# A fused two-block transformer kernel: experts of the second stage sorted by token count, with 96, 64 or 32 slots by rank

## The reference, cut to what matters

```
g_top_p, g_top_i = lax.top_k(softmax(t @ rg_w + rg_b), 1)
e_top_v, e_top_i = lax.top_k(expert logits of that group, 2)
w_top = softmax(e_top_v) * g_top_p
for e in range(16):
    hid = silu(t @ w_gate[e]) * (t @ w_up[e])
    out = out + combine[:, e:e + 1] * (hid @ w_down[e])
```

## Time and profile before

| what | value |
|---|---|
| runs | 1474.21, 1475.78, 1477.21 us |
| profiled execution, first to last instruction | 1474.6 us |
| TensorE busy over the span | 1431.9 us, 97% |
| second expert stage, from its first gate matmul | 1210.4 us on |
| its last down matmuls end | 1463.5 us |

### The profile page before, as it was taken

The page is one execution under the profiler, slowest core; times in us unless marked ns, Lnnn a source line. Parts: engine busy times, 40 slices in busy tenths (PEclk is TensorE's granted clock), DMA queues, the critical chain, the costliest instruction groups (busy, mean ns, idle before and its releaser), DMA issues.

```text
span 1474.6 us, 19938 instructions
## 1 busy us (share of the span) xinstructions
PE 1431.9 (97%) x8514; PEld 986.2 (67%) x8514; DVE 605.8 (41%) x1228; ACT 224.1 (15%) x430; POOL 18.0 (1%) x44
## 2 busy tenths in 40 slices
PE   9999999999999999999999998989999999999996
PEld 7888888688888886555455444446788876455542
DVE  1557998989963252222221211115123251211222
ACT  0220100411112023110111010102122022111011
POOL 0000000000000000001000000000010000000000
PEclk9999999999999999999999999999999999999999
DMA  9731223864343768999999999995654658999975
GB/s 382 319 120 58 101 85 120 351 235 177 117 171 139 326 277 326 385 426 416 426 425 428 428 428 427 426 427 220 191 217 162 258 232 323 427 427 427 426 308 247
DMA packets 37198, 435.48 MB, mean 295 GB/s; under 512 B 4449, under 2 KB 5865, under 8 KB 10873
## 3 DMA queue, kind: packets, MB, share of 16 engines
q1 hardware_dynamic: 34272, 427.89, 71.2%
q0 software_dynamic: 1664, 4.52, 0.9%
q10 hardware_dynamic: 1176, 1.84, 0.8%
HBM read 431.61 MB, written 2.62 MB: 294 GB/s over the span
## 4 chain that ended last, share of the span: by engine, by line
PE 84%; DMA 13%; DVE 1%; ACT 0%; issue 0%; SPq 0%; POOL 0%; ACTq 0%; DVEq 0%; POOLq 0%
PE PP L880 21%; PE PP L1221 18%; PE PP L1236 9%; PE MB L1010 7%; DMA ZC<-in_w_moe 6%; PE MB L1205 5%; DMA KQ<-in_w_moe 5%; PE PP L1034 3%; PE MB L1008 3%; PE PP L918 3%; DMA RA<-in_w_moe 2%; PE PP L950 2%; PE PP L1197 1%; PE MB L1060 1%; PE PP L868 1%; PE MB L950 1%
## 5 line engine op out<-in xcount | busy, mean ns | idle before, releaser
L880 PE MATMUL PP<-uT,ring 128*128 128x256 f32 x704 | 153.2, 379 | 0.0
L880 PEld LDWEIGHTS PP<-uT,ring 128*128 128x128 f32 x704 | 133.4, 190 | 18.5 <-issue 0.5
L1947 DVE TENSOR_SCALAR wctx<-wctx 128x1 f32<-128x1 f32 x50 | 7.7, 154 | 304.4 <-PE PP L1221 304.4
L1494 DVE SCALAR_TENSOR_TENSOR ZC<-ZC,vec 128x256 f32<-128x256 f32 x240 | 116.2, 484 | 7.8
L1221 PE MATMUL PP<-ring,const 128*64 128x256 f32 x992 | 112.4, 380 | 5.5 <-DMA ring<-in_w_moe 4.8
L1205 PE MATMUL MB<-V 64*128 64x512 f32 x400 | 112.1, 639 | 1.7 <-DVE V L1970 0.9
L1221 PEld LDWEIGHTS PP<-ring,const 128*64 128x64 f32 x992 | 71.8, 137 | 48.6 <-issue 9.0
L1962 DVE SCALAR_TENSOR_TENSOR V<-V,wctx 128x256 f32<-128x256 f32 x100 | 48.5, 485 | 114.7 <-PE MB L1205 100.0
L740 ACT ACTIVATE V<-PP 128x256 f32<-128x256 f32 x50 | 19.2, 384 | 376.4 <-PE PP L1221 376.4
L1236 PE MATMUL PP<-ring,const 128*64 128x512 f32 x320 | 73.1, 598 | 0.6 <-ACT const L748 0.6
L1221 PE MATMUL PP<-ZC,const 128*64 128x256 f32 x512 | 59.9, 388 | 4.9 <-DMA ZC<-in_w_moe 4.6
(11 more groups left out here) (477 smaller groups left out, 2034.2 us busy)
## 6 DMA issues: line engine op xcount, KB each, us to landing
ring<-in_w_moe SPq DMA_DIRECT2D x53, 2048.0 KB, 17.4
RA<-in_w_moe SPq DMA_DIRECT2D x20, 2048.0 KB, 14.3
ZC<-in_w_moe SPq DMA_DIRECT2D x20, 2048.0 KB, 16.2
Vc<-in_w_moe SPq DMA_DIRECT2D x17, 2048.0 KB, 17.5
KQ<-in_w_moe SPq DMA_DIRECT2D x17, 2048.0 KB, 19.5
extra<-in_w_moe SPq DMA_DIRECT2D x17, 1792.0 KB, 15.1
ring<-in_w_ada SPq DMA_DIRECT2D x12, 2048.0 KB, 10.6
ring<-in_w_gates SPq DMA_DIRECT2D x7, 2048.0 KB, 7.8
```

The lines of the kernel that those rows point to most:

```text
L880: ins = pe.matmul(out[:, c, :], W[:, k * width + at:k * width + at + P], X[:, k, :], start=k == 0, stop=k == K - 1)
L1494: ins = V_.scalar_tensor_tensor(conv[:, t, :], zpad[:, t, k:k + L], tap, conv[:, t, :], ALU.mult, ALU.add)
```

## The change

Only the second expert stage changes what it does; `PLANS[0]` of the first stage is again 31 windows of 64. In the second stage:

- Experts 0, 1, 2 stay steps 0, 1, 2, with 64, 64 and 96 slots. The other 13 are ranked on VectorE by token count (`sort_experts`), and steps 3 to 14 take the ranks of `RANK_OF`, the last loop's first pass the smallest expert (rank 12, 64 slots). The largest has 96 slots, ranks 1 to 5 have 64, ranks 6 to 11 have 32.
- 96 slots are a wide window ("M", 64 rows, as before) and a narrow one ("N", 32 rows) in one step, with the same weights. A narrow window is 32 columns of stationary operand in four column groups of the array: gate and up are 32 matmuls each of 128 moving columns (before 16 of 256), down is 16 of 256 (before 8 of 512), the turn is 1 transpose (before 2), the scatter 8 matmuls of 256 columns from 32 rows each, in two halves, each of which waits until what was scattered before is complete.
- The weights of steps 3 to 14 are loaded at an address from a register, which SyncE loads from the table (line 503); the first of these loads waits for the sort.
- Overflow is counted beyond each expert's own capacity, and the placing numbers use the step's base and capacity.

The diff, cut to its core:

```diff
-SLOTS = 64
+SLOTS, NARROW = 64, 32
+FIXED, LAST_RANK = 3, 12
+RANK_OF = (11, 10, 9, 8, 0, 1, 2, 3, 4, 7, 6, 5)
+def plan(n):
+    if n == 0:
+        kinds = ["M"] * (EXPERTS[0] - 1)
+    else:
+        kinds = ["M", "M", "MN"] + ["MN" if r == 0 else "M" if r <= 5 else "N" for r in RANK_OF]
...
+def scattered_with(n, w):
+    return sum(2 if kind == "M" else 8 for step in PLANS[n] for v, kind, _ in step if v <= w)
...
             def load(w):
+                block = s[x["b"]]
+                if x["src"] == "moe1" and x["b"] >= 3 * FIXED:
+                    step = x["b"] // 3
+                    if x["b"] % 3 == 0:
+                        if step == FIXED:
+                            sp.wait_ge(moe[1]["items_ready"], 2)
+                        expert[0] = sp.value_load(tab[0:1, 40 + step:41 + step], min_val=0, max_val=EXPERTS[1] - 1)
+                    block = s[bass.ds(3 * expert[0] + x["b"] % 3, 1)].rearrange("a p n -> p (a n)")
...
+                def scatter_n(part, before):
+                    if before:
+                        pe.wait_ge(m["scattered"], before)
+                    for t, g in ((part, 0), (part, 2), (1 - part, 1), (1 - part, 3)):
+                        rows = slice(NARROW * g, NARROW * (g + 1))
+                        pe.matmul(acc[t][g // 2][:, (g % 2) * L:(g % 2 + 1) * L], S_n[rows, t * P:(t + 1) * P], ys_n[rows, :],
+                                        start=False, stop=False, tile_position=(NARROW * g, 0)).then_inc(m["scattered"], 1)
...
+                def gate_or_up_n(out, W):
+                    for k in range(DT):
+                        for g in range(4):
+                            ins = pe.matmul(out[NARROW * g:NARROW * (g + 1), :], xs_n[:, k, :], weights(W, k * 512 + g * P, P),
+                                            start=k == 0, stop=k == DT - 1, tile_position=(0, NARROW * g))
...
+                def down_n(k, W):
+                    pe.wait_ge(m["ht_ready"], k + 1)
+                    for c in range(4):
+                        for g in range(4):
+                            ins = pe.matmul(y_n[NARROW * g:NARROW * (g + 1), :], hts_n[:, NARROW * c:NARROW * (c + 1)],
+                                            weights(W, c * D + g * L, L), start=c == 0, stop=c == 3, tile_position=(0, NARROW * g))
...
                     w_wait(pe, ju["w"])
-                    gate_or_up(1, W_of(ju), xs if k else xsc[:, :, 0:SLOTS]).then_inc(job_done, 1)
+                    for _, kind, _ in steps[k]:
+                        if kind == "M":
+                            ins = gate_or_up(1, W_of(ju), xs if k else xsc[:, :, 0:SLOTS])
+                        else:
+                            pe.wait_ge(m["y_kept"], steps[k - 1][-1][0] + 2)
+                            ins = gate_or_up_n(up_n, W_of(ju))
+                    ins.then_inc(job_done, 1)
...
+                def sort_experts():
+                    link(V_.scalar_tensor_tensor(o_("key"), r_("cnt")[:, FIXED:E], float(E), iota[:, 0:R], ALU.mult, ALU.subtract))
+                    link(V_.tensor_tensor(order_of, along(o_("key")), across(o_("key")), ALU.is_gt))
+                    link(V_.tensor_reduce(o_("rank"), order_of, AX.X, ALU.add))
+                    link(V_.tensor_tensor(order_of, along(o_("rank")), across(cst("step_rank", R)), ALU.is_equal))
+                    link(V_.tensor_tensor(order_by, order_of, along(iota[:, FIXED:E]), ALU.mult))
+                    link(V_.tensor_reduce(o_("ids"), order_by, AX.X, ALU.add))
+                    V_.tensor_copy(tab[0:1, 40 + FIXED:40 + E - 1], o_("ids")[0:1, 0:R - 1])
+                    V_.tensor_copy(tab[0:1, 72:73], o_("ids")[0:1, R - 1:R]).then_inc(m["items_ready"], 1)
...
-                link(V_.tensor_scalar(e_("ovf"), e_("cnt"), float(SLOTS), None, ALU.is_gt))
-                for c in (2, 3):
-                    link(V_.scalar_tensor_tensor(e_("ovf"), e_("cnt"), float(c * SLOTS), e_("ovf"), ALU.is_gt, ALU.add))
+                assigned_rows(0)
+                assigned_rows(1)
+                if n == 1:
+                    sort_experts()
+                assigned_rows(2)
+                assigned_rows(3)
+                room = e_("cnt")
+                if n == 1:
+                    sorted_places()
+                    room = e_("t1")
+                    link(V_.tensor_tensor(room, e_("cnt"), o_("cap"), ALU.subtract))
+                first_over = 0 if n == 1 else 1
+                link(V_.tensor_scalar(e_("ovf"), room, float(first_over * SLOTS), None, ALU.is_gt))
+                for c in range(first_over + 1, 4):
+                    link(V_.scalar_tensor_tensor(e_("ovf"), room, float(c * SLOTS), e_("ovf"), ALU.is_gt, ALU.add))
```

More of the change, by code:

```diff
@@ L51, with capacity @@
 ROUTE_WAIT, RANK_WAIT, ROWS_WAIT = 16, 6, 12
-SLOTS = 64
+SLOTS, NARROW = 64, 32
[6 more added lines that the diff above has]
+        kinds = ["M", "M", "MN"] + ["MN" if r == 0 else "M" if r <= 5 else "N" for r in RANK_OF]
+    steps, last, w = [], {"M": 0, "N": 0}, 0
+    for kind in kinds:
+        steps.append([])
+        for x in kind:
+            steps[-1].append((w, x, w - last[x]))
+            last[x] = w
+            w += 1
+    return steps
+PLANS = [plan(n) for n in range(2)]
+WINDOWS = [sum(len(x) for x in steps) for steps in PLANS]
+def scattered_with(n, w):
+    return sum(2 if kind == "M" else 8 for step in PLANS[n] for v, kind, _ in step if v <= w)
+def capacity(step):
+    return sum(SLOTS if kind == "M" else NARROW for _, kind, _ in step)
 QH, HD = 8, 64
@@ L437, in _ @@
         def _(sp):
+            expert = [None]
             def load(w):
@@ L1255, in gather_more, with steps_before, scatter_step, turn_step @@
                         gather(unit // 2, unit % 2, spread[0 if unit >= 6 else unit % 2])
+                steps = PLANS[n]
+                def steps_before(step):
+                    return steps[steps.index(step) - 1] if step is not steps[0] else []
+                def scatter_step(step, part):
+                    both = len(step) == 2
+                    w, kind, _ = step[part if both else 0]
+                    if part == 0 or both:
+                        pe.wait_ge(m["y_kept"], w + 2)
+                        pe.wait_ge(m["s_ready"], w + 1)
+                    before = scattered_with(n, w - 1)
+                    if kind == "N":
+                        for half in range(2) if both else (part,):
+                            scatter_n(half, before + 4 * half)
+                        return
+                    if part == 0 and "N" in (x for _, x, _ in steps_before(step)):
+                        pe.wait_ge(m["scattered"], before)
+                    for half in range(2) if both else (part,):
+                        scatter(half, "scattered" if half else None, first=w == 0)
+                def turn_step(step):
+                    for w, kind, _ in step:
+                        if kind == "M":
+                            turn_hidden(w)
+                        else:
+                            turn_hidden_n(w)
                 for k in range(E - 1):
@@ L1293, in route_and_experts @@
                     w_wait(pe, jd["w"])
-                    down(k, W_of(jd)).then_inc(job_done, 1)
+                    for w, kind, _ in steps[k]:
+                        if kind == "M":
+                            ins = down(w, W_of(jd))
+                        else:
+                            ins = down_n(w, W_of(jd))
+                    ins.then_inc(job_done, 1)
                     if k == 1 and n == 0:
                         gather_more((7,))
-                        pe.wait_ge(m["y_kept"], k + 1)
-                        pe.wait_ge(m["s_ready"], k)
-                        scatter(0, first=True)
-                        scatter(1, "scattered", first=True)
+                        scatter_step(steps[0], 0)
+                        scatter_step(steps[0], 1)
                 wg, wu, wd = (bays[x] for x in tail_bays(n))
@@ L1885, in route, with assigned_rows @@
                 of_tokens(r_("pos"))
-                for c in range(4):
+                def assigned_rows(c):
                     if c:
@@ L1971, in keep_y, with keep_y_n @@
                     ins.then_inc(m["y_kept"], 1)
+                def keep_y_n():
+                    V_.tensor_copy(ys_n, y_n).then_inc(m["y_kept"], 1)
+                steps = PLANS[n]
                 for k in range(E - 1):
@@ L1974, in route @@
                         job_wait(dve, J[f"moe{n}", 3 * k + 1, 0])
-                        hidden(k)
-                        dve.wait_ge(m["scattered"], 2 * k)
-                        placing(k)
+                        for w, kind, since in steps[k]:
+                            step_hidden(w, kind, since)
+                        dve.wait_ge(m["scattered"], scattered_with(n, steps[k - 1][-1][0]))
+                        for w, kind, _ in steps[k]:
+                            if kind == "M":
+                                placing()
```

(12 more changed lines are left out.)

191 lines of the change are left out of this document (142 added, 49 removed).

## The result

The changed kernel takes 1452.91 us (median of 4 runs, 1451.39 to 1456.64), the kernel before 1474.99 in the same measurement: ratio 0.9849, 95% interval 0.9837 to 0.9862. That is 22 us less, where 34 were forecast. The direction and the mechanism hold, but the time lies 11 us above the 1442 of the forecast. The profiled execution (1454.33 us, span 1452.5) shows where.

A forecast was written before the change was run, and what follows sets the result against it. Before, TensorE and DMA were both full, TensorE never waiting. After, DMA's end at 1439.8 us, later than TensorE's 1434.5, plus 1.2 for register loads gave 1441, 1442 as median; own range 1435 to 1450, 8-in-10 range 1434 to 1464.

The forecast's parts named there:

- the first rival: Narrow matmuls bound by their number, records no closer than 56 ns, gate and up 3.5 us each: 1462 us; chance 0.2.
- Windows, passes, weights: Second stage: 18 windows, 10 wide and 8 narrow, one loop pass, 16 sets of weights, two fewer than before.
- Price of a narrow window: Second stage, TensorE: narrow gate, up and down 1.8 us each; a narrow step 7.9 us, with residual 8.5.
- The scatter half: Narrow window: 0.85 us for each half of the scatter, eight records, against an array share of 0.43.
- TensorE's sum: Second stage from step 2 through the loop pass: 172.5 us on TensorE, giving its end alone at 1434.5 us.
- The late start: Sort adds 5.7 us on VectorE before the second stage's first hidden rows; everything behind on TensorE starts 3.4 us later.
- The DMA end: Second stage: 31 loads of 4.92 us from 1269.5, last landing 1425.1, then down 3.6 and 11.1: 1439.8 us.
- The waits before the end: Second stage: TensorE first waits for a load at the gate of step 14, some 3.4 us.
- Waits between engines in a narrow window: Rival: each of eight narrow windows costs 2.5 us more, less the slack of 5: 1456 us; chance 0.09.
- Loads not hidden: Rival: 32-column weight loads not hidden at all, a narrow window costs 12 us more: 1531 us; chance 0.06.
- T = 2: Rival: an overflow is left, adding one loop pass of 14.7 us: 1456 us; chance 0.02.
- The clock: Rival: TensorE gets half the clock in short steps, some 50 us of narrow steps near double: about 1485; chance 0.03.

The follow-up runs named there:

- the run with half loads: The changed kernel with only half the bytes loaded in the nine loads of fixed steps 12, 13 and 14, all matmuls kept: 1440.96 us.
- the second profile: The changed kernel measured and profiled once more without any edit: 1450.91 us, ratio 0.9835.
- kernel with the table of its own: The changed kernel with its 46 new constants in a separate input and tile behind all others, old tiles at their old places: 1445.67 us.
- the run with wide windows: The changed kernel with its six narrow single windows (steps 3 to 6, 12, 13) made wide, double steps kept: 1471.20 us.
- padded kernel: The kernel before with 46 unused columns more in its table of constants, nothing else changed: 1481.80 us, ratio 1.0045.
- two columns more: The changed kernel with the first hidden rows made early and two unused columns more in the table of constants: 1444.52 us.
- first hidden rows early: The changed kernel with the second stage's first hidden rows made ahead of VectorE's last placing instructions and diagonal matrices: 1449.32 us.

## Why the prediction was right and where it was wrong

The forecast had the right two engines, the right direction and the right end: the stream of weights ends last, TensorE has slack. Its sum was 3.5 us too small at the end of the stream, and 5 us in the attention block were not in it at all. The time lies outside the forecast's own range (to 1450) and inside its wide one, to 1464, only because that reached to the first rival, whose cause was not there; that part is luck.

**Windows, passes, weights.** Right: 10 wide, 8 narrow, T = 1.

**Price of a narrow window.** Right, and the choice near the lower bound was good: 1.75 us for gate and down, 1.86 for the up. The Trainium skill ("TensorE: Matmul & The Clock Gate", Part 3) would have the weight load beside a matmul in flight only when the row group differs. Here all groups share the rows, each record has a weight load of 110 ns, and the records stand 26 ns apart, below the 56 ns that the first rival needed. This trace does not agree with the sentence. The scatter half was set too high (0.85 for 0.65); it lies halfway between the router's records and the array's share of 0.43.

**TensorE's sum.** 172.5 us was 6 too much: the run with half loads takes 171.5, and some 166.5 without its pause and the low clock behind it. The six single narrow steps, forecast at 8.5 with the residual and measured at 7.6, are 5.5 of it.

**The late start.** VectorE's added work is 5.7 us, as forecast. From the first product of the `G` matrices to the first hidden rows it takes 1231.91 - 1213.31 = 18.60 us; before it was 1218.29 - 1205.40 = 12.89. Timeline of VectorE, the change twice, then before:

```profile
1213.31 0.69 DVE L2051 TENSOR_TENSOR const<-const,biasr 128x512 f32<-128x512 f32 x1
...
1231.91 0.42 DVE L2166 TENSOR_TENSOR const<-PP,V 128x256 f32<-128x256 f32 x1
```

```profile
1205.40 0.69 DVE L1889 TENSOR_TENSOR const<-const,biasr 128x512 f32<-128x512 f32 x1
```

What is left on TensorE is 3.4 us in the second profile (40.53 against 37.11), as forecast.

**The DMA end: the first step that failed, 3.5 us.** The kernel with the table of its own shows it, since its gate of step 2 stands at 1251.04, where 1250.9 was forecast. Load 17 was issued at 1270.29 (1269.5 forecast). The last load but one, `ZC`, should then land after 30 x 4.92 + 3.1 us, at 1421.0; TensorE got it at 1423.50. So 2.5 us are missing, and the windows show some 2 of them at the start, 243 GB/s where 426 were counted:

```profile
1265.00:1270.00 5.00, 5.00 (x52) 2.04 (x52) 2.50 (x6) 0.00 (x0) 0.00 (x0) 1.00 0.84 338
1270.00:1275.00 5.00, 5.00 (x140) 4.00 (x132) 1.47 (x4) 0.70 (x2) 0.00 (x0) 1.00 0.77 243
1275.00:1420.00 145.00, 134.05 (x1709) 78.93 (x1707) 31.22 (x76) 14.47 (x37) 0.00 (x0) 0.98 1.01 426
```

And the end does not hang on the last down's load, as the sum had it. Timeline of TensorE in the last pass of the same kernel:

```profile
1423.50 3.67 PE L1322 MATMUL PP<-ZC,const 128*64 128x256 f32 x32 [1.19 <-DMA ZC<-in_w_moe]
...
1428.27 0.44 PE L1352 MATMUL PP<-const 128*128 128x128 f32 x2
...
1429.70 3.65 PE L1359 MATMUL PP<-ring,const 128*64 128x512 f32 x16
```

The down follows the up, scatter and turn without a wait. From the landing of `ZC` to the end of the span it is 21.0 us; the sum had 14.7 from a landing 4.9 later, 19.6. Together the later issue, the missing rate and the longer tail are 0.8 + 2.5 + 1.4 = 4.7 us. The 1.2 that were added for register loads cost nothing that shows, which leaves 3.5. So 1442 becomes 1445.5, and this kernel takes 1445.67.

**The waits before the end.** That the first wait for a load stands at step 14, some 3.4 us, was wrong: two waits stand in step 13 already, at its gate and its up, and the sum is three times as large. TensorE's slack was put at 5.3 us (1439.8 - 1434.5); with the 4.7 above and the 6 of the sum, less the pause of 2.4, it is 13.6, as the run with wide windows gives (13.5). The waits cost nothing beyond the loads' own end. By its own signs the forecast would also be wrong if TensorE waited in steps 3 to 7 or a narrow step took over 9 us. Step 5 does both, with the pause: 10.3 us. The other narrow step with the residual, step 4, takes 7.6, and the pause was in no term of the sum.

**The size that was missed: 5 to 6 us outside the diff's stage.** The forecast costed the 46 constants at nothing, or rather not at all. They moved every tile behind the table, the write of `relb_d` took 46 us instead of 42.5, its reads were issued just ahead of the next load of weights and landed late. VectorE, which before began 2.6 us after the usual landing of the last read (1085.0 against 1079.6 + 2.8), had to wait, TensorE behind it stood still for 3.4 us and ran some 2 us longer at the low clock. This is the larger part of what is missing: 1450.91 - 1445.67 = 5.2 us in the change (5.9 when each is taken against the kernel before in its own measurement) and 6 in the padded kernel before. The remaining 2 us of the first measurement (1452.91 against 1450.91) are spread between measurements; no cause is shown for them.

**The rivals.** None of them has the cause. Narrow records bound by number: refuted by 26 ns. Waits between engines in a narrow window: 0.16 us between scatter halves, 0.3 in two waits. Loads not hidden, T = 2: no. The clock: in the change it falls within the narrow steps only where TensorE waits for loads anyway (0.89 from 1400 to 1430 us); in two of the experiments (half loads, and two columns more) it fell behind the pause too, for some 7 us.

## What to carry to other kernels

When a change makes one engine of a stage cheaper, read at once where the other one ends: here six narrow windows take 34 us off TensorE, of which 20 show. What was still won here came from an earlier start, before the stream of weights was without gaps (1210 to 1275 us). When a change adds to a tile that others lie behind, list the DMAs that read or write the moved tiles and whose slack is small; new constants belong behind everything else, or padded to the old offsets. An end that hangs on a stream of loads is to be computed from each of the last landings with the work that follows it, not from the last landing alone.

## What was not expected of the hardware

- *The rate of DMA changes with the byte offset of a tile.* With four of the nine bays 32 bytes past a multiple of 64, full streams of 2 MB loads move 424 GB/s, at 64 past a multiple of 128 they move 426, at a multiple of 128 they move 428. The write of `relb_d`, 1024 rows of 1536 bytes, takes 42.4 to 42.8 us with its source at a multiple of 128 (five profiles), 46.1 to 46.8 at 32 past one (eight) and 45.8 at 64 past one (one). The source rows of the write start 0, 32 or 64 past a multiple of 128, and also 0, 160 or 192 past a multiple of 256, so these runs do not tell which power counts. Where the 3.7 us arise is open: from 1040 to 1045 us, in which it runs alone or nearly so, it moves 51 GB/s before (166 to 168 rows in the five profiles) and 49 in the padded kernel (154 to 159 rows in seven of the eight, 166 in the first profile of the change). Over all 1024 rows that would be 1.3 to 1.8 us; the rest falls where the write shares the engines with weights.
- *A pause inside a run of narrow matmuls.* In all kernels with narrow steps 4 and 5 it stands behind the 55th of the 64 records of the up of step 5 and lasts 1.3 to 2.5 us; with wide steps there it is gone. No engine and no load of weights releases it. In the change the instruction queue fetched twice from 1285 to 1300 us (packets, MB, share of the DMA engines):

```profile
q8 instruction: 2, 0.03, 0.8%
```

A narrow step issues in 7.6 us more matmuls and weight loads than a wide one in 13.6, while DMA is full. The Trainium skill ("Runtime: NRT & Kernel Launch", Instruction fetch mechanics) has the engine's own queue fetch blocks of 256 instructions ahead and calls the cost mostly hidden; that the pause is such a fetch fits its fixed place. The traces say more: in all seven kernels with the pause one packet of the instruction queue starts 2.3 to 2.5 us before TensorE goes on, whatever the length of the pause. In the change it starts at 1297.85 us, TensorE goes on at 1300.24, and the pause is 2.47 us; with the first hidden rows early it starts at 1291.20, and the pause is half as long:

```profile
1293.68 0.49 PE L1327 MATMUL PP<-KQ,const 128*32 128x128 f32 x9 [1.26 <-issue]
```

So the pause is as long as this packet is late, as it would be if TensorE had run out of instructions; no run moved a fetch to prove it. In the change the pause cost no time, since the loads set the end; with half loads it did, and the low clock behind it.
